# Expert loop on PE: down product and gather of the neighbouring experts placed between up steps, two weight buffers, loop body of four

## The reference

```
def hier_moe(h, wg, bg, we, be, w_up, w_down):
    ...                                   # one of 4 groups, then top 2 of its 8 experts
    def run_block(args):
        xb, e = args                      # 1024 wide rows of the tokens of expert e
        gu = xb @ w_up[e]                 # 1024 -> 2 x 512
        return (jax.nn.silu(gu[:, :EXPERT_FF]) * gu[:, EXPERT_FF:]) @ w_down[e]   # 512 -> 1024
    ...                                   # rows times gate, added to their tokens
```

## Time and profile before

| | us |
|---|---|
| median of 3 runs | 1510.23 (1510.15 to 1515.94) |
| the profiled execution | 1516.76 |
| its span, first to last instruction | 1515.1 |
| expert loop of layer 0, of layer 1 | 347 to 811, 1035 to 1499 |

### The profile page before, as it was taken

One profiled execution on the slowest core, in us unless ns is written; L12 is line 12 of the kernel. 1 busy time (PEld: TensorE's weight loads), 2 busy tenths in 40 slices (PEclk: granted clock), 3 DMA queues, 4 the chain that ended last, 5 costly groups with the idle time before them and its releaser, 6 DMA issues.

```text
span 1515.1 us, 31030 instructions
## 1 busy us (share of the span) xinstructions
PE 1400.2 (92%) x13378; PEld 675.5 (45%) x13378; DVE 486.1 (32%) x1260; ACT 276.0 (18%) x749; POOL 124.3 (8%) x179
## 2 busy tenths in 40 slices
PE   7999998789999998999996899988999998999996
PEld 4578898453333332333333665644333332333332
DVE  3726565533112122122122443423122122122123
ACT  3224232210111111111112241110111111111111
POOL 3000686000000000000001010100000000000000
PEclk9999999988999999999998898997999999999999
DMA  9523200669999999999987154279999999999991
GB/s 339 149 79 110 72 4 4 204 278 390 427 425 427 425 428 420 427 426 425 427 340 227 43 146 160 82 291 383 427 427 425 426 427 425 425 425 425 427 403 41
DMA packets 72834, 464.36 MB, mean 306 GB/s; under 512 B 12322, under 2 KB 33052, under 8 KB 45372
## 3 DMA queue, kind: packets, MB, share of 16 engines
q1 hardware_dynamic: 71052, 456.00, 74.2%
q0 software_dynamic: 1648, 6.33, 1.6%
HBM read 455.72 MB, written 6.59 MB: 305 GB/s over the span
## 4 chain that ended last, share of the span: by engine, by line
PE 89%; DVE 6%; issue 2%; ACT 2%; DMA 0%; POOL 0%; POOLq 0%; DVEq 0%; SPq 0%; ACTq 0%
PE bank L1278 31%; PE bank L1264 12%; PE bank L766 10%; PE bank L1291 8%; PE bank L1064 6%; PE bank L1340 4%; PE bank L1129 3%; PE bank L966 2%; PE bank L1271 2%; DVE arena L1849 2%; PE bank L960 1%; PE bank L736 1%; PE bank L936 1%; PE bank L816 1%; PE bank L984 1%
## 5 line engine op out<-in xcount | busy, mean ns | idle before, releaser
L1278 PE MATMUL bank<-slot,arena 128*32 128x256 f32 x2816 | 340.6, 631 | 12.3 <-issue 11.2
L1264 PE MATMUL bank<-h,arena 128*32 128x256 f32 x1536 | 190.5, 641 | 1.2 <-DVE arena L1845 1.2
L1278 PEld LDWEIGHTS bank<-slot,arena 128*32 128x32 f32 x2816 | 96.6, 123 | 205.7 <-issue 195.4
L1278 PE MATMUL bank<-arena 128*32 128x256 f32 x1280 | 154.0, 632 | 0.0
L1857 DVE SCALAR_TENSOR_TENSOR arena<-arena,bank 128x128 f32<-128x128 f32 x64 | 18.5, 289 | 366.2 <-ACT arena L1471 364.4
L1484 ACT COPY arena<-bank 32x256 f32<-32x256 f32 x252 | 91.7, 364 | 153.0 <-PE bank L1291 150.8
L1264 PEld LDWEIGHTS bank<-h,arena 128*32 128x32 f32 x1536 | 61.3, 129 | 115.2 <-issue 113.7
L1471 ACT ACTIVATE arena<-bank 128x128 f32<-128x128 f32 x64 | 17.8, 279 | 466.7 <-PE bank L1278 466.7
L581 POOL TENSOR_SCALAR arena<-arena 128x1 f32<-128x1 f32 (+2 forms) x18 | 4.6, 257 | 1110.9 <-ACT h L1459 1071.2
L2255 DVE TENSOR_TENSOR x<-bank,x 128x512 f32<-128x512 f32 x64 | 44.1, 692 | 154.1 <-PE bank L1340 153.8
L1291 PE MATMUL bank<-slot,arena 128*32 128x256 f32 x1408 | 85.1, 382 | 0.7 <-ACT arena L1475 0.7
(11 more groups left out here) (405 smaller groups left out, 1531.0 us busy)
## 6 DMA issues: line engine op xcount, KB each, us to landing
slot<-in_exp_w_up SPq DMA_DIRECT2D x88, 2048.0 KB, 17.0
slot<-in_exp_w_down SPq DMA_DIRECT2D x44, 2048.0 KB, 17.2
arena<-in_exp_w_up SPq DMA_DIRECT2D x40, 2048.0 KB, 18.3
mixedT<-in_exp_w_down SPq DMA_DIRECT2D x20, 1024.0 KB, 16.5
hT<-in_exp_w_down SPq DMA_DIRECT2D x20, 1024.0 KB, 12.2
slot<-in_w_in SPq DMA_DIRECT2D x6, 1536.0 KB, 7.0
slot<-in_w_out SPq DMA_DIRECT2D x4, 2048.0 KB, 8.4
slot<-in_w_in SPq DMA_DIRECT2D x3, 2048.0 KB, 9.6
```

What stands on the lines that cost most here:

```text
L1264: last = pe.matmul(ps[0][strip * CAP:(strip + 1) * CAP, 0:DW], G[:, t, :], h[:, t, :].rearrange("p (f k) -> p k f", k=KT)[:, strip * (DW / ...
L1278: last = pe.matmul(ps[bank][strip * CAP:(strip + 1) * CAP, 0:2 * FW], xs[:, c, strip_k * CAP:(strip_k + 1) * CAP], up_cols(wup[slot_j], k, ...
```

## The change

In `expert`, the products of neighbouring experts are placed between the up steps: behind step 2 the activation's transpose of the expert before, behind step 3 its down product, behind step 4 the gather for the next expert, behind step 5 the transpose of the gathered rows. The five sums stand behind steps 4 to 8, the placing transposes behind step 6. The copied transpose `xs` has two buffers; the fallback's row buffer `ynat` loses one. `m_used` is split into `m_up` and `m_down`. Buffers 0 and 1 take turns, and the third serves expert 2 of each layer only; PE's loop has one quad in its body and six passes. DVE's order follows PE's. Layer 1's keys load after the last expert, the first two parts of its input weights in front of them. The fallback's eight steps become a loop on every engine.

```diff
-            def up_k(slot_j, k, bank):
+            def up_k(slot_j, k, bank, par=0):
...
-                    last = pe.matmul(ps[bank][...], xs[:, c, strip_k * CAP:(strip_k + 1) * CAP],
+                    last = pe.matmul(ps[bank][...], xs[par][:, c, strip_k * CAP:(strip_k + 1) * CAP],
...
-                        n = k - 2                      # sum_between
+                        n = k - 3
...
-                        if k == 2:                     # places_between
+                        if k == 5:
...
+                def activated(e):
+                    pe.wait_ge(s["m_act"], base + e + 1)
+                    act_T(s["m_actT_ps"])
+
+                def down(e, sl, par, loaded, started=True):
+                    pe.wait_ge(s["m_actT"], base + e + 1)
+                    if started:
+                        pe.wait_ge(s["m_nat"], base + e - 1)
+                    pe.wait_ge(s[f"wdn{sl}"], 2 * loaded if sl == THIRD else loaded)
+                    for f in range(FF // 128):
+                        down_f(sl, f, 6 + par).then_inc(s["m_down"], 1)
+
+                def expert(e, sl, par, loaded, prev, between=lambda k: None, final=False):
+                    pe.wait_ge(s["m_xs"], base + e + 1)
                     for k in range(KT):
                         if k % (KT // 2) == 0:
                             pe.wait_ge(s[f"wup{'ab'[k // (KT // 2)]}{sl}"], loaded)
-                        up_k(sl, k, 2 + par).then_inc(s["m_used"], 1)
+                        up_k(sl, k, 2 + par, par).then_inc(s["m_up"], 1)
+                        if k == 1 and prev:
+                            activated(e - 1)
+                        if k == 2 and prev:
+                            down(e - 1, *prev)
+                        if k == 3 and not final:
+                            pe.wait_ge(s["m_G"], base + e + 2)
+                            gather(s["m_xg_ps"])
+                        if k == 4 and not final:
+                            pe.wait_ge(s["m_xn"], base + e + 2)
+                            x_T(s["m_xT_ps"])
                         between(k)
-                    ...                                # gather, act_T, x_T, down_f stood here
...
+                expert(0, 0, 0, loads[0] + 16, None)
+                expert(1, 1, 1, loads[1] + 16, (0, 0, loads[0] + 16, l > 0))
+                expert(2, THIRD, 0, 16 * (l + 1), (1, 1, loads[1] + 16, l > 0), places_between(0, l == 0))
+                expert(3, 0, 1, loads[0] + 32, (THIRD, 0, 16 * (l + 1)))
...
-                with pe.Fori(0, 2) as i:
-                    for n in range(3):
-                        quad(3 * i + n + 1, 4 * (n + 1), 4 * i)
-                quad(QUADS - 1, 4 * (QUADS - 1), 0, final=True)
+                with pe.Fori(1, QUADS - 1) as g:
+                    quad(g)
+                quad(QUADS - 1, final=True)
+                activated(NE - 1)
+                down(NE - 1, 0, 1, loads[0] + 32 * QUADS)
...
-                with sp.Fori(1, NE // RING) as i:      # SP
-                    for j in range(RING):
-                        refill(RING * i + j, j, RING * i + j - RING)
-                for e in range(NE // RING * RING, NE):
-                    refill(e, e % RING, e - RING)
+                refill(3, 0, 0)
+                refill(4, 1, 1)
+                with sp.Fori(2, NE // 2 - 1) as i:
+                    refill(2 * i + 1, 0, 2 * i - 1)
+                    refill(2 * i + 2, 1, 2 * i)
+                refill(NE - 1, 0, NE - 3)
...
                 def quad(g, first=False, final=False):  # DVE
                     for j in range(4):
                         it = base + 4 * g + j
-                        if j == 0 and not first:
-                            quad_sums(g - 1)
-                        if j == 2:
-                            quad_places_T(g)
-                        dve.wait_ge(s["m_tanh"], it + 1)
-                        swiglu(2 + j % 2, (s["m_q"], it), s["m_act"])
+                        sums = j == 0 and not first
+                        if j > 0 or not first:
+                            dve.wait_ge(s["m_tanh"], it)
+                            swiglu(2 + (j + 1) % 2, (s["m_q"], it - 1), s["m_act"])
                         if not (final and j == 3):
                             dve.wait_ge(s["m_xg_ps"], it + 2)
                             xn_out(s["m_xn"])
+                        if sums:
+                            quad_sum(g - 1, 0)
+                        if not (final and j == 3):
                             dve.wait_ge(s["m_xT_ps"], it + 2)
-                            xs_out(s["m_xs"])
+                            xs_out(s["m_xs"], (j + 1) % 2)
+                        if sums:
+                            for n in range(1, SUMS):
+                                quad_sum(g - 1, n)
+                            dve.wait_ge(s["m_add"], SUMS * (quads + g))
                         if not (final and j >= 2):
                             onehot(4 * g + j + 2, 0, s["m_G"])
                         if j == 1:
                             quad_places(g)
+                        if j == 2:
+                            quad_places_T(g)
```

More of the change, by code:

```diff
@@ L39 @@
 SUMS = 5
-RING = 3
-LOADS = [len(range(j, NE, RING)) for j in range(RING)]
 LAST_SUMS = [(0, 4), (1, 5), (4, 6), (2, 7), (3, 0)]
@@ L213, in build @@
         xn = carve(DW)
-        xs = carve(DW).rearrange("p (c n) -> p c n", c=DW // 128)
+        xs = [carve(DW).rearrange("p (c n) -> p c n", c=DW // 128) for _ in range(2)]
         actT = carve(FW).rearrange("p (c n) -> p c n", c=FW // 128)
@@ L217, in build @@
         an = carve(FW)
-        ynat = [carve(DW) for _ in range(2)]
+        ynat = carve(DW)
         S4 = carve(3 * 4 * CAP).rearrange("p (t j n) -> p t j n", t=3, j=4)
@@ L703, in _ @@
                     with pool.Fori(0, NE) as e:
[L704 to L707, removed]
+                        with pool.Fori(0, STEPS_REST) as b:
+                            write_rows(rows_rest[l], e * RROWS + CAP * b, rest_at(STEPS_REST * e + b, "nat"), s[f"r_act{l}"], s[f"ryw{l}"])
+                    pool.wait_ge(s[f"ryw{l}"], 16 * STRIPS * STEPS_REST * NE)
                     for k in range(2):
@@ L1272, in x_T @@
                 last.then_inc(s_done, 1)
-            def up_k(slot_j, k, bank):
+            def up_k(slot_j, k, bank, par=0):
                 strip_k, c = divmod(k, DW // 128)
                 for strip in range(STRIPS):
-                    last = pe.matmul(ps[bank][strip * CAP:(strip + 1) * CAP, 0:2 * FW], xs[:, c, strip_k * CAP:(strip_k + 1) * CAP],
+                    last = pe.matmul(ps[bank][strip * CAP:(strip + 1) * CAP, 0:2 * FW], xs[par][:, c, strip_k * CAP:(strip_k + 1) * CAP],
                                      up_cols(wup[slot_j], k, strip), start=(k == 0), stop=(k == KT - 1))
@@ L1374, in expert @@
                             pe.wait_ge(s[f"wup{'ab'[k // (KT // 2)]}{sl}"], loaded)
-                        up_k(sl, k, 2 + par).then_inc(s["m_used"], 1)
-                        between(k)
[L1377 to L1392, removed]
-                    for j in range(4):
[L1395 to L1398, removed]
-                        if j == 2:
-                            between = places_between(g, places_first)
-                        expert(4 * g + j, sl, j % 2, 16 * (LOADS[sl] * l + 1) + 16 * (turn + (c + j) // RING),
-                               started=sums or j >= 2 or l > 0, final=final and j == 3, between=between)
@@ L1404, in _ @@
-                quad(0, 0, 0, places_first=l == 0, sums=False)
+                        up_k(sl, k, 2 + par, par).then_inc(s["m_up"], 1)
[9 more added lines that the diff above has]
+                            x_T(s["m_xT_ps"])
@@ new lines, in expert, with quad @@
+                        between(k)
+                loads = [16 * (NE // 2) * l, 16 * (NE // 2 - 1) * l]
+                def quad(g, final=False):
+                    at = [loads[1] + 32 * g, loads[0] + 32 * g + 16, loads[1] + 32 * g + 16, loads[0] + 32 * g + 32]
+                    prev = (0, 1, loads[0] + 32 * g)
+                    for j in range(4):
+                        sl = 1 - j % 2
+                        between = (sum_between(g - 1), lambda k: None, places_between(g), lambda k: None)[j]
+                        expert(4 * g + j, sl, j % 2, at[j], prev, between, final and j == 3)
+                        prev = (sl, j % 2, at[j])
@@ L1414, in _ @@
                     with pe.Fori(0, NE) as e:
-                        pe.wait_ge(s[f"rw{l}"], 64 * (e + 1))
-                        for b in range(STEPS_REST):
+                        with pe.Fori(0, STEPS_REST) as b:
                             it = STEPS_REST * e + b
+                            pe.wait_ge(s[f"rw{l}"], 64 * (e + 1))
                             pe.wait_ge(r("dve"), rest_at(it, "G") + 1)
@@ L1475, in actT_out, with nat_out @@
                 act.copy(actT.rearrange("p c n -> p (c n)"), ps[5][:, 0:FW]).then_inc(s_done, 1)
```

(17 more changed lines are left out.)

41 lines of the change are left out of this document (18 added, 23 removed).

## The result

The changed kernel takes **1489.85 us** (median of 4 runs, 1487.86 to 1499.57) against 1510.34 (1510.15 to 1515.94): a ratio of 0.987, 95% interval 0.982 to 0.992. It is 20 us faster. The forecast was 1573 us, slower; what came is its rival A in mechanism, though A's own figure was 1503 us.

The account below looks back on a forecast made before the run. PE was taken as the bound, by little. Jumps +56, down product and gather -6, step-2 wait +17, skip -4, buffers 0 sum to +63 us: 1573 us against the median; own range 1545 to 1596, overall range 1495 to 1596.

Parts of the forecast that it names:

- rival A: PE's jumps back: the target is still kept, so no jump costs anything; 1503 us, 1480 to 1516, chance 0.24.
- The step that failed: PE's loop body of four: each jump back must fetch its target at 7.0 us, +56 us in all.
- Down product and gather between up steps: Expert loop on PE: the old 0.29 us wait goes, new places cost little; -0.1 per expert, -6 us (-29 to +19).
- The wait at step 2: PE waits for VectorE's activation after each expert carrying a quad's five sums: 14 x 1.2 = +17 us, bounds 0 to 28.
- Rival C: The wait at step 2 comes in every expert, not one in four: 24 us more, 1597 us; chance 0.04.
- Two buffers: Weight stream gives up 10 us of lead after experts 3 and 4: 0, up to +6 us if jumps cost nothing.
- The hole behind expert 4: Weight stream stops after experts 3 and 4; the fill for 5 starts about 43 us into the loop, not 33.
- Skip and layer's end: PE's jump over the shrunken fallback code gets cheaper, up to 7.5 us, taken as -4; reordered layer-end loads cost nothing.

## Why the prediction was wrong

*The step that failed* is "I read this as: PE holds the packet it runs and the next. A target four packets back is gone." That packets come one at a time shows how far PE fetches ahead. It says nothing of how long a packet that has run stays, and the trace of before could not: its one jump in each layer went back some twelve packets. The runs show the edge: four and six packets stay, seven and eight do not. So ten jumps cost nothing instead of 70 us, and the term was -14 instead of +56. The kernel before without its jumps, faster by 14 us in its loops, confirms the price of a jump that has to fetch; only how many of them would was wrong. The Trainium skill ("Runtime: NRT & Kernel Launch", "Instruction fetch mechanics") has two statements on this. Its 128 KiB for PE goes with a body of six packets that is kept, but not with one of seven, by its 16 KiB blocks an estimate of 112 KiB, which was fetched anew. Its window of two pages, out of which a jump costs a fetch, does not hold for the jumps back here, over four and six packets. The 0.24 for rival A was too low for a reading that rested on no row of a jump whose target was four packets back.

*Down product and gather between up steps:* right in direction, too small. Three buffers with the pipeline against the kernel before, both written out, is -2.6 us a loop with the wait in it. Without the wait (14.7 us, from the run that moved the add) that makes -20 us, against -6 in a range of -29 to +19. The plain expert went from 12.90 to 12.60 us, the 0.29 us of the old wait; the added places cost no more than the old ones. The -0.1 per expert was put "nearer to the low end" of -0.45 to +0.30, but it is the middle; -0.3 was measured.

*The wait at step 2:* +17 was forecast, 14.7 measured behind the sums and 2.1 at the layers' ends: 1.05 us each, in the experts named. Rival C is out: in plain experts the activation is there.

*Two buffers:* 0, up to +6 if the jumps cost nothing; it was +7.7, the loops of the changed kernel against those with three buffers. This holds two things, as the run with three buffers fetches its code: +15.6 for the buffers with code fetched in both, and 7.8 less as the kept body fetches none. The hole behind expert 4 was as described: the fill for expert 5 starts 43.6 us into the loop, where 43 was forecast, and at 20 MB the stream is 9 us behind the one with three buffers, where 10 was. That it would cost something only with free jumps was right, and this is what happened. What the sum left out is what follows from it: once the stream sets the end, PE's gains come back as waits for weights. In the changed kernel the moved add is worth 3.2 us by both loops (0.8 by the medians, of different rounds), with three buffers 8.0 (8.7 by the medians).

*Skip and layer's end:* -4 was forecast, -8 measured, just past the bound of 7.5. 5.9 of it is the skip, by the run that unrolls the steps again: without them no gap stands there, and the low clock behind it goes as well. The other 2 stay open.

So the sum by what was measured, both layers: -14 (jumps) -20 (pipeline) +15 (wait) +8 (buffers and kept body) -8 (skip and layer's end) = -19, against -20.5 by the medians. Its terms are steps along a chain of runs from before to after, so that they add up to the table is no proof; each rests on its own run. Rival A had the mechanism, but its 1503 us lies 13 above the result, since the pipeline and the skip gave more than it had and the buffers took more. The ranges were narrower than the terms' bounds: added up, these give 1530 to 1613 us for the forecast, not 1545 to 1596, and 1460 to 1549 for A, not 1480 to 1516. The result lies outside the forecast either way.

## What to carry to other kernels

On PE a jump back was free or dear by whether its target was still kept, so a loop body is a size to be tried on the chip; how far code is fetched ahead doesn't tell it. When two resources are full at once, a wait taken off one is worth little while the other has no lead: the same moved add gave 3 us with two buffers and 8 with three. So read the other resource's waits beside each gain. And a time that fits a theory is no proof where a run without the cause takes the same time; look for the row that the theory alone would leave. Where unchanged code moves by several microseconds between executions, compare segments between named rows, not totals.

## What the runs showed of the hardware

PE kept loop bodies of four and six packets of code (67 and 71 packets in all) and fetched bodies of seven and eight anew (163 and 115), with about nine packets a pass for seven. A jump that misses left a gap of 5.0 us behind a down product and 3.5 behind up steps, both with the DMA at 426 GB/s, and 2.1 us with the DMA at 0; only in the first two did the clock stand at 0.50 behind it. Why the gap is 1.5 us shorter behind up steps wasn't tried. And code costs the stream something, too: 427 against 429 GB/s with 40 packets more, and the last weights of a loop land 4 us later, over their last 3 us at half of the DMA's share.
